# Mixer state stage ahead of the pooling, first copies of an attention step ahead of other ScalarE work, last gate products in four banks, single last stores

## What is computed

```python
for i in range(2):                                   # the two layers
    proj = x @ w_in[i]                               # q, k, v of two attentions, gates
    ya = neighbourhood_attention(q_na, k_na, v_na, rpb)
    yb = bidirectional_retention(q_r, k_r, v_r, g_r, decay_f, decay_b)
    merged = sigmoid(gate_a) * (ya @ w_a) + sigmoid(gate_b) * (yb @ w_b)
    x = layer_norm(ALPHA * x + merged @ w_out, ...)
    ffn = (gelu(conv(x @ w_up)[a]) * conv(x @ w_up)[b]) @ w_down
    ple = sigmoid(x @ w_ple_gate) * (p[i] @ w_ple_proj)
    x = layer_norm(ALPHA * x + ffn + ple, ...)
u = rmsnorm(x) @ w_in_2                              # the mixer
y_pool = pool_mixer(u[:, :512])      # trailing means over 2, 4, 8, 16 tokens, 4 products
y_ssm = ssm_mixer(u[:, 512:])        # linear state recurrence, gelu, y * sigmoid(y @ w_glu)
x = x + concat(y_pool, y_ssm) @ w_out_2
x = x + swiglu(rmsnorm(x))
return rmsnorm(x)
```

## Time and profile before

| quantity | value |
|---|---|
| median of 3 runs | 2344.29 us (2343.88 to 2344.67) |
| the profiled execution | 2344.25 us, its span 2342.5 us |
| PE busy | 2292.3 us, 98% of the span |
| DVE, ACT, POOL busy | 974.4, 976.0, 1152.9 us (42%, 42%, 49%) |
| share of the 16 DMA engines of the main queue | 27.5% |
| mean granted TensorE clock | 0.995 of full |

### The profile page before, as it was taken

The page is one execution under the profiler, slowest core; times in us unless marked ns, Lnnn a source line. Parts: engine busy times, 40 slices in busy tenths (PEclk is TensorE's granted clock), DMA queues, the critical chain, the costliest instruction groups (busy, mean ns, idle before and its releaser), DMA issues.

```text
span 2342.5 us, 32502 instructions
## 1 busy us (share of the span) xinstructions
PE 2292.3 (98%) x11672; PEld 1892.0 (81%) x11672; DVE 974.4 (42%) x1607; ACT 976.0 (42%) x1376; POOL 1152.9 (49%) x706
## 2 busy tenths in 40 slices
PE   8999999999999999999999999999999989999998
PEld 7888888888888886888888888888887768888886
DVE  6355343343544205544453352433376675222201
ACT  5444343244555325443443343555513434443321
POOL 3433325577984455333334464444455755444452
PEclk9999999999999999999999999999999999999999
DMA  5222222222323432222222223323333112323331
GB/s 206 79 66 84 87 81 99 93 88 95 95 84 117 126 97 72 81 77 89 69 81 90 93 81 100 101 92 100 107 99 108 46 46 90 98 90 98 99 99 54
DMA packets 61140, 214.18 MB, mean 91 GB/s; under 512 B 7184, under 2 KB 7440, under 8 KB 61072
## 3 DMA queue, kind: packets, MB, share of 16 engines
q1 hardware_dynamic: 58336, 205.11, 27.5%
q10 hardware_dynamic: 2736, 8.14, 1.1%
HBM read 211.13 MB, written 2.10 MB: 91 GB/s over the span
## 4 chain that ended last, share of the span: by engine, by line
PE 93%; DVE 4%; ACT 1%; issue 1%; POOL 1%; DMA 0%; SPq 0%; ACTq 0%; DVEq 0%; POOLq 0%
PE psum L830 85%; PE psum L858 2%; PE psum L859 2%; PE psum L863 1%; PE psum L961 1%; DVE states L2238 1%; PE psum L949 1%; PE psum L928 1%; POOL xl L683 0%; DMA stage<-in_w 0%; PE psum L1228 0%; PE psum L1017 0%; PE psum L1054 0%; DVE pr L1878 0%; DVE states L2252 0%
## 5 line engine op out<-in xcount | busy, mean ns | idle before, releaser
L461 POOL TENSOR_TENSOR w_lo<-stage,w_hi 128x1024 fp32r<-128x1024 f32 x378 | 920.9, 2443 | 1100.4 <-ACT w_hi L1368 1086.3
L830 PE MATMUL psum<-xh,w_hi 128*128 128x512 f32 x1712 | 671.5, 392 | 5.5 <-DVE na_q_lo L1845 5.5
L830 PE MATMUL psum<-xl,w_hi 128*128 128x512 f32 x1712 | 666.9, 390 | 0.0
L830 PE MATMUL psum<-xh,w_lo 128*128 128x512 f32 x1712 | 666.4, 389 | 0.0
L1368 ACT ACTIVATE w_hi<-stage 128x1024 fp32r<-128x1024 f32 x377 | 396.7, 1053 | 353.3 <-PE psum L830 349.1
L830 PEld LDWEIGHTS psum<-xh,w_hi 128*128 128x128 f32 x1712 | 321.3, 188 | 77.6 <-DVE na_q_lo L1845 8.2
L830 PEld LDWEIGHTS psum<-xh,w_lo 128*128 128x128 f32 x1712 | 321.3, 188 | 67.8
L830 PEld LDWEIGHTS psum<-xl,w_hi 128*128 128x128 f32 x1712 | 321.5, 188 | 64.6
L830 PE MATMUL psum<-g_hi,w_hi 128*128 128x512 f32 x528 | 206.2, 391 | 0.0
L830 PE MATMUL psum<-g_hi,w_lo 128*128 128x512 f32 x528 | 205.4, 389 | 0.0
L830 PE MATMUL psum<-g_lo,w_hi 128*128 128x512 f32 x528 | 205.4, 389 | 0.0
(11 more groups left out here) (401 smaller groups left out, 3384.6 us busy)
## 6 DMA issues: line engine op xcount, KB each, us to landing
stage<-in_w SPq DMA_DIRECT2D x379, 512.0 KB, 3.5
bias_raw<-in_bias ACTq DMA_DIRECT2D x8, 384.0 KB, 3.0
out_x<-out_t SPq DMA_DIRECT2D x4, 512.0 KB, 2.7
z<-in_x SPq DMA_DIRECT2D x3, 512.0 KB, 7.1
p_raw<-in_p ACTq DMA_DIRECT2D x2, 512.0 KB, 3.6
masks_raw<-in_masks SPq DMA_DIRECT2D x1, 576.0 KB, 10.3
masks_raw<-in_masks ACTq DMA_DIRECT2D x1, 576.0 KB, 5.1
stage<-in_w ACTq DMA_DIRECT2D x1, 512.0 KB, 4.8
```

The costliest lines, as they stand in the source:

```text
L461: pool.tensor_tensor(w_lo[s][:, :, :], stage[s][:, :, :], w_hi[s][:, :, :].bitcast(F32), ALU.subtract).then_inc(lo_done, 1)
L830: mm = pe.matmul(dst, lhs[i], rhs[j], start=start and n == 0, stop=stop and n == 2)
```

## The change

Eight edits. (1) The 8 KB `decay` load goes from SP's queue to ACT's, ahead of ACT's load of unit 1, and the three activations on it go ahead of the first weight rounding. (2) In every attention step ACT makes the copy of unit 0 first, then `round_ahead(L, 0)`, the wait for `xl` and the bias load, and the Exp dummy comes later. (3) In the second layer unit 1's high passes start one tile later and stretch further (`steps`). (4) The last four PLE products use `PLE_BANK`. (5) In the mixer's first norm ACT takes the root ahead of a weight rounding. (6) POOL's pooling begins only when all four state tiles are done; PE takes unit 7 and GLU behind the states, then the state half MS with the pool products between its units, then the pooled half MP, now four units. (7) `second_norm` sends its sums two tiles later and its spread one later. (8) The last two output tiles are stored singly.

```diff
@@ sp @@
-            sp.dma_start(decay[:], a["decay"]).then_inc(decay_in, 16)
...
-            for first in range(0, KT, 2):
-                sp.wait_ge(normed, MIX * 2 * KT + (first + 2))
...
+            for first, end in ((0, 2), (2, 4), (4, 6), (6, 7), (7, 8)):
+                sp.wait_ge(normed, MIX * 2 * KT + end)
@@ gpsimd @@
-            pooling(0)
             mixer_low(8)
-            pooling(1)
             mixer_low(9)
-            pooling(2)
-            mixer_low(10)
-            pooling(3)
-            for u in range(11, GU_U0):
+            pool.wait_ge(state_im, SP_T)
+            for g in range(SP_T):
+                pooling(g)
+                mixer_low(10 + g)
+            for u in range(10 + SP_T, GU_U0):
                 mixer_low(u)
@@ tensor @@
-                first_units(L, 0, 0, L * 2 * KT, ui, ri, lags=(0, 5) if L else (2, 4))
+                first_units(L, 0, 0, L * 2 * KT, ui, ri, steps=(1, 2, 3, 4, 5, 7, 8, 9) if L else range(2, KT + 2))
...
-                    dst = take_bank(L, PLE_R0 + KT + m)
+                    pe.wait_ge(ple_term, L * KT + (m + 1))
...
                 in_unit(6, take_bank(MIX, MIN_R0 + 6))
+                block_inputs(3)
+                convolve(1)
                 from_state(0)
-                block_inputs(3)
+                from_state(1)
+                convolve(2)
+                convolve(3)
+                from_state(2)
+                from_state(3)
                 in_unit(7, take_bank(MIX, MIN_R0 + 7))
...
+                half_units(GLU_U0, GLU_R0, 2, *ssm_y)
                 pool_product(0)
                 pool_product(1)
...
+                half_units(MS_U0, MS_R0, 4, *ssm_mix, inside=pooled_products, together=True)
+                half_units(MP_U0, MP_R0, 4, *pool_mix)
 
                 def second_norm(k):
-                    if k == 4:
+                    if k == 6:
                         mean_square(n0 + 1, rstd_2, sq_2[(KT - 1) % 4])
-                    if k == KT:
+                    if k == KT + 1:
                         spread(n0 + 1, rstd_2)
@@ scalar @@
-                act.activation(warm[:, :], ln_eps[:, :], ACT.Exp)
+                copy_blocks(0, na_q[:, :], NA_DH ** -0.5, block_view(U_BANK[0][:, :])).then_inc(na_hi, 1)
+                round_ahead(L, 0, ui)
+                act.wait_ge(x_lo, (L * 2 + 1) * KT)
                 act.wait_ge(unit_used, L * LAYER_U + t * 12 + 1)
...
-                ahead(1)
                 b_apart(BT - 1)
                 b_apart(BT - 2)
                 root(n0, rstd_1, (square_mean, 1))
+                ahead(1)
                 ahead(2)
...
+            act.dma_start(decay[:], a["decay"]).then_inc(decay_in, 16)
             act.dma_start(stage[1][:, :, :].rearrange("p t n -> p (t n)"), a["w"][1]).then_inc(landed[1], 16)
```

More of the change, by code:

```diff
@@ L1258, in pool_product @@
                 def pool_product(g):
-                    dst = take_bank(MIX, WP_R0 + g)
                     if g == 0:
                         pe.wait_ge(wp_in, 16)
+                    pe.wait_ge(y_skip, g + 1)
                     pe.wait_ge(pooled, 2 * g + 2)
[L1263 to L1273, removed]
-                            pe.wait_ge(*ready(k))
-                            mm = passes(dst[:, :], wt(u, 4 * (m % 2) + k), parts(k), k == 0, k == SP_T - 1)
-                        mm.then_inc(unit_used if m % 2 else mid_done, 1)
@@ L1278, in mixer, with half_units @@
-                pool_mix = ((lambda k: (mix_lo_s, k + 1)), (lambda k: (mix_hi[:, k, :], mix_lo[:, k, :])))
-                ssm_mix = ((lambda k: (mix_lo_s, SP_T + k + 1)), (lambda k: (mix_hi[:, SP_T + k, :], mix_lo[:, SP_T + k, :])))
+                    pe.matmul(Y[g][:, :], w_pool[:, g, :], u_all[:, g, :], start=True, stop=True).then_inc(pool_done, 1)
+                def half_units(u0, r0, count, ready, parts, inside=lambda u: None, together=False):
+                    for u in range(count):
+                        take_unit(MIX, u0 + u)
+                        order = [(h, k) for h in range(2) for k in range(SP_T)]
+                        if together and u == 0:
+                            order = [(h, k) for h in range(2) for k in range(SP_T - 1)] + [(h, SP_T - 1) for h in range(2)]
+                        for h, k in order:
+                            if k == 0:
+                                take_bank(MIX, r0 + 2 * u + h)
+                            pe.wait_ge(*ready(k))
+                            mm = passes(U_BANK[(r0 + h) % 2][:, :], wt(u0 + u, 4 * h + k), parts(k), k == 0, k == SP_T - 1)
+                            if k == SP_T - 1:
+                                mm.then_inc(unit_used if h else mid_done, 1)
+                        inside(u)
@@ L1660, in mixer @@
                     if m % 2 == 0:
[L1661 to L1662 removed]
+                        ahead(MP_U0 + m // 2)
+                    square(n0 + 1, m, sq_2, after(MP_R0 + m))
                     act.activation(xh[:, m, :], z[:, m, :], ACT.Copy,
@@ L2323, in mixer, with ssm_half @@
                     dve.tensor_tensor(y, y, glu_sig[m % 2][:, :], ALU.mult).then_inc(y_ssm, 1)
-                for m in range(4, KT):
-                    mix_low(m)
-                    pool_half(m)
+                def ssm_half(m):
+                    add_half(m, MS_R0 + m, MS_U0 + m // 2, MS_M0 + m // 2)
+                skip(0)
+                skip(1)
+                skip(2)
+                yg_low(0)
+                skip(3)
+                yg_low(1)
+                yg_low(2)
+                yg_low(3)
+                gated(0)
+                gated(1)
+                mix_low(4)
+                gated(2)
+                mix_low(5)
+                gated(3)
+                mix_low(6)
+                mix_low(7)
+                ssm_half(0)
+                ssm_half(1)
+                mix_low(0)
+                mix_low(1)
+                ssm_half(2)
+                ssm_half(3)
+                mix_low(2)
+                ssm_half(4)
+                ssm_half(5)
+                mix_low(3)
+                ssm_half(6)
+                ssm_half(7)
                 def scaled_low(k):
```

172 lines of the change are left out of this document (72 added, 100 removed).

## The result

| | before | after |
|---|---|---|
| median | 2344.48 us (4 runs, 2343.88 to 2345.67) | 2325.43 us (4 runs, 2324.25 to 2327.12) |
| ratio | | 0.9918 (0.9907 to 0.993) |
| profiled execution | 2344.25 us | 2327.12 us, span 2325.3 |
| PE, DVE, ACT, POOL busy | as above | 2291.1, 964.4, 975.7, 1153.7 us |

Faster by 19.0 us (0.8%) in the medians and by 17.1 between the two profiled executions, where 23.0 was forecast. The profiled execution of after is the slowest of its four, so terms are compared with 17.1.

What follows compares the result with a forecast made beforehand. PE, busy 98% of the span, bounds the kernel, so gains come from its waits at stage joints or its clock. Terms 11.3 + 1.1 + 4.0 + 1.9 + 2.7 + 0.8 + 0.8 + 0.4 = 23.0 us give 2321.2, range 2316 to 2331.5.

Steps and rivals of the forecast that it cites:

- rival (a): Mixer: POOL's chain becomes the bound, 6 us more wait and 1.6 us of slow clock, 2328.9 us; chance 0.20 including part.
- 7.0 + 1.0 + 1.6 + 2.4 of waits: Mixer: PE's old waits for states and pooling, then for the pooled half's inputs, in us, were to vanish.
- 1.6 of slow clock: Mixer: loss from 3.5 us at clock 0.52 right after the 2.4 us wait, counted as gone.
- new are 2.5: Mixer: a new PE wait of about 2.5 us, split between pooled for the last product and unit 13's low part.
- 1.5 us lost to DVE: Mixer: delay allowed in POOL's chain for DVE, making unit 13's low part ready at 1927.6.
- The rule on the port: Mixer: DVE and GpSimd share a port pair locked per whole instruction; by it the sum would be 6.5 us worse, 2327.7.
- the 40.6 of its own work: Mixer: POOL's four pooling groups, 31 us in all, plus four low parts of 2.4 us.
- the rule's 8: Mixer: up to 8 us lost as pooling takes turns with 16 GLU and split subtractions of about 0.5 us.
- It takes the 1.8 away: Start: moving the decay activations ahead removes unit 2's 1.8 us delay, but makes the first matmul later; net 0.8 us.
- rival (c): Start: decay lands late, 5 us less gain, 2326.5 us; chance 0.10 shared with rival (d).
- rival (d): Attention: moved roundings make unit 3 late, 5.9 us of gain gone, 2327 us; chance 0.10 shared with rival (c).
- the bound of 0: Last store, half as large: lower bound of its gain, 0.4 us forecast with bounds 0 and 1.3.

Runs made afterwards that it cites:

- the pooling not held back: Changed kernel with POOL's pooling in its old place, not waiting for the state tiles, PE's new order kept; 2335.07 us, 0.9958.
- five small edits undone: Changed kernel with decay load and activations, unit 1's high passes, first-norm root, second-norm sums and spread, and last stores as before; 2329.22 us, 0.9935.
- first copy behind again: Changed kernel with unit 0's copy again behind table load and rounding, decay activations just before unit 2's rounding, second-norm spread a step earlier; 0.9929.
- POOL's low parts in the gaps: Changed kernel with only POOL's order changed: group 0 after low part 8, low parts 9 and 10 after two and three state tiles; 2318.72 us, 0.9887.
- start, spread and first unit: Changed kernel with decay load and activations as before, second-norm spread one tile earlier, first state unit input tile by input tile; 2324.30 us, 0.9915.
- the next kernel: Changed kernel with group 0 between low parts 8 and 9, unit 7 earlier, old decay placement, earlier spread, first state unit by input tiles; 2321.64 us, 0.9901.
- one group first: Changed kernel with pooling of group 0 ahead of low parts 8 and 9, low part 10 first behind the states; 2323.95 us, 0.991.
- the best version: Changed kernel with low parts 9 and 10 and group 0 between state tiles, old decay placement, earlier spread, first state unit by input tiles; 2317.26 us, 0.988.
- group 0 between two low parts: Changed kernel with group 0 between low parts 8 and 9, low part 10 after the states, unit 7 ahead of the last from_state; 2325.06 us, 0.9913.

## Why the prediction was right, and which terms were not

The range of 2316 to 2331.5 held; 2325.4 lies 0.4 above the band (2317 to 2325) to which I gave 0.62. Seven of the eight edits gave 10.5 us where I had 11.7. The term that was mis-sized is edit 6, 11.3 forecast and 5.8 measured, and what happened there is a part of rival (a).

| term | forecast | measured | where |
|---|---|---|---|
| edit 6 | 11.3 | 5.8 | last matmul of `in_unit(6)` to the second norm's `first_units`: 97.0, 91.2 us |
| edits 2, 3, steps | 4.0 | 4.0 | 12.23, 10.91 us, three times |
| edit 2, first step | 1.9 | 1.8 | 14.80, 13.01 us |
| edit 4 | 2.7 | 3.0 | 1.5 in each layer |
| edit 5 | 1.1 | 0.6 | sums to spread 4.51, 3.87 us |
| edit 1, start | 0.8 | 0.7 | unit 2 at 22.90, 22.24 |
| edit 7 | 0.8 | 0.4 | 13.88, 13.44 us |
| edit 8 | 0.4 | 0.0 | first `out_t` (2334.02, 2316.82) to end of span 8.48 us in both |

That makes 16.3. The mixer's first stretch at half clock in the kernel before, 1.5 us, is not there after, and the last spread runs at half clock only after (2.07 us instead of 1.16): 16.9 of the 17.1.

**Edit 6.** Its main steps hold. The tiles do shrink to 9.9 us; without the wait for the states they are slow again (the pooling not held back). POOL's chain is late next at unit 12 and 13, and for 2.9 us where 2.5 was worked out. What failed is the sentence on the sum, "gone are 7.0 + 1.0 + 1.6 + 2.4 of waits, 0.2 of refill and 1.6 of slow clock, 13.8; new are 2.5". I counted POOL's turns with DVE on POOL's side only ("1.5 us lost to DVE"), and not that DVE's splits behind the gates are stretched from 0.69 to 2.84 us: two waits of 1.5 us, 1.8 with refill. And I took the half clock as gone, while the new waits have one behind them: from 1919.33 to 1925.45, 15 starts 0.43 apart instead of 0.227, 2.9 us. POOL's two waits cost 3.2 with refill, and three gaps of 0.3 to 0.4 behind the pool products 1.1: in all 9.0 us are lost after, start to start, where I had 2.5, against 14.0 before. That would make 5.0, but the 1.1 is no new loss: without their waits the eight matmuls of the pool products hold PE for 3.7 us before and for 2.7 after, since the gap then stands behind them. Without it 7.9 us are lost after, which makes 6.1 for the stage's 5.8. In the length of the half clock there was bad luck: the runs with five small edits undone and with the first copy behind again have the same instructions in this stage and 3.4 us of half clock instead of 6.8, and take 89.7 and 89.9 us, so edit 6 is worth 5.8 to 7.3. Taking the low parts and group 0 out of the splits' way gives 8.3 us back in this stage (91.2 to 82.9) and full clock.

**The rule on the port.** I had weighed the rule of the Trainium skill (SBUF — State Buffer, section SBUF: two separate sides), an exclusive lock held for a whole instruction against DVE instructions with two SBUF inputs, and said that POOL's rows bear it out in part only. The traces bear out that the two engines take turns over whole instructions: a DVE instruction beside a 2.4 us low part takes 2.84 to 2.87 us, its products from PSUM 0.69, and a low part behind DVE's unbroken line 4.82. POOL's line from the end of the states to the low part of unit 13 is 46.0 us (1873.3 to 1919.3), 5.4 over the 40.6 of its own work, between my 1.5 and the rule's 8.

**The start.** 0.7 is near 0.8, but for another reason. "It takes the 1.8 away" was wrong of edit 1: it is edit 2 that does so (2.2 us), through the same turn-taking, and edit 1 takes 1.5 back. So the right size was luck. The first matmul comes at 8.89, 1.45 later and not 1.0, since the activations hold ACT until 6.35, with `decay` landing after 3.5 us; rival (c) is out.

**Attention and PLE.** Sizes right. Which edit gives what is now known: edit 3 all of the three later steps, edit 2 the first. No wait appeared at unit 3, so rival (d) is out.

**Small ones.** Edit 5 gives 0.6 between the traces and 0.9 in the run that undoes it: ACT's four splits start at 1817.31, with PE's sums, and end at 1819.76, 0.5 behind them, where I had them end first. Edit 7 gives back 0.65, not 0.5, and the spread at KT is right. Edit 8: 256 KB land in 2.7 us like 512 KB, the bound of 0 that I gave. By the formula of the Trainium skill (DMA: Bandwidth & Descriptors, section Anatomy of one DMA), an estimate, the gain would have been 0.6. That section is on DMAs that GpSimd issues; these stores are SP's, and for them the 2.7 us of both sizes decides.

## What to carry to other kernels

Where two engines share something they take turns on, price the wait on both sides, and look which of the two has other work to cover it: here 6.7 us came from moving one group of the pooling and two subtractions on POOL, with no work removed. Order an engine by windows in which its neighbour does not need the shared thing (a semaphore at the start of such a window does it), not by when its own inputs are ready. When several edits touch one wait, undo them one by one: the decay edit had the right sign in the sum and was itself a loss.

## What the runs showed of the hardware

- DVE and POOL take turns in these DVE operations, which have all their inputs in SBUF: sums and products (0.68 to 2.87 us), splits (0.69 to 2.84), a scaling by a column (0.68 to 2.83), scans (eight in 2.62, up to 6.15). A statistics step on 128x6 kept its 0.15. With an input in PSUM they do not: in five traces (before, after, five small edits undone, the pooling not held back, POOL's low parts in the gaps) all 440 executions of the operation on `conv_a` and `psum` took 0.74 to 0.75 us, and 403 of them began while POOL was at work.
- A DVE line without gaps kept its speed (0.68 each) and the low part beside it took 4.82 us; a low part that had started first took 2.84 instead of 2.40, and the DVE instruction 2.84 to 2.87.
- The half-clock stretches in the mixer began in or behind waits of PE. In four kernels of four (after, five small edits undone, first copy behind again, and start, spread and first unit) the pair of waits of 1.75 to 2.50 and of 1.1 us was followed by 3 to 7 us at half clock; a single wait of 1.12 us at that place was not, nor one of 1.83 for `mix_lo` with the pooling not held back. The waits of 1.32 and 1.81 us for `yg_lo` were followed by 6.8 us, those of 0.64 and 1.14 in the next kernel by none. The wait of 1.87 us ahead of the mixer is followed by one in some traces (before, first copy behind again, one group first) and not in others (after, the best version). The four times of the kernel with group 0 between two low parts lie 11 us apart, with mean granted clocks of 0.995 in the slower two and 0.998 in the faster; 0.003 of 2320 us is some 7 us, an estimate of what the clock has in that. Only one execution of each kernel has a trace.
- A store of 256 KB from SP's queue lands in 2.7 us, like one of 512 KB.
